# Block one's small inverses: transposed matrices by VectorE's block transpose, and seven more input pages in high and low halves

## The reference, cut to what matters

```python
h = rms_norm(x, norm1_g[l])
proj = h @ w_in[l]
p_rwkv, p_sb, q_mem, gate_logits = jnp.split(proj, cut, axis=-1)
...
def step(S, inp):                     # one token of the recurrence, 8 heads of 64 x 64
    r_t, w_t, k_t, v_t, kk_t, a_t = inp
    sa = jnp.einsum('bhij,bhj->bhi', S, -kk_t)
    S = S * w_t[:, :, None, :] + sa[..., None] * (kk_t * a_t)[:, :, None, :] + v_t[..., None] * k_t[:, :, None, :]
    y_t = jnp.einsum('bhij,bhj->bhi', S, r_t)
    return S, y_t
```

## Time and profile before

| | us |
|---|---|
| median of 3 runs (1365.85 to 1368.22) | 1367.03 |
| the profiled execution, whole time | 1366.13 |
| its span in the trace | 1364.3 |
| TensorE busy in it | 1269.6 |
| VectorE, ScalarE, GpSimd busy | 811.6, 673.0, 569.9 |

### The profile page before, as it was taken

How to read it: one execution, slowest core, us unless ns; L and a number is a source line. 1 busy time by engine, 2 the same in 40 slices (tenths; PEclk the granted TensorE clock), 3 DMA queues, 4 the chain that set the end, 5 groups by cost and what they waited for, 6 DMA issues and landing times.

```text
span 1364.3 us, 22840 instructions
## 1 busy us (share of the span) xinstructions
PE 1269.6 (93%) x8934; PEld 910.7 (67%) x8934; DVE 811.6 (59%) x1854; ACT 673.0 (49%) x1501; POOL 569.9 (42%) x385
## 2 busy tenths in 40 slices
PE   9999999999999999999999988888889888888786
PEld 7988897989999999997896543333434333333232
DVE  5845202464568773457338776666677666667755
ACT  4710233646566665564325564454555444554544
POOL 1100023516878888740005444444434444444342
PEclk9999999999999999999999999999999999999999
DMA  7432322425645556557539999999999999999997
GB/s 265 140 100 90 110 90 75 131 93 171 200 158 188 181 186 200 157 163 267 222 105 414 420 421 422 422 421 421 421 422 422 422 421 421 421 422 422 422 422 302
DMA packets 67940, 381.10 MB, mean 279 GB/s; under 512 B 7552, under 2 KB 7552, under 8 KB 35200
## 3 DMA queue, kind: packets, MB, share of 16 engines
q0 software_dynamic: 37296, 268.45, 47.4%
q1 hardware_dynamic: 29664, 107.84, 24.1%
q10 hardware_dynamic: 880, 3.41, 0.7%
HBM read 378.63 MB, written 1.05 MB: 278 GB/s over the span
## 4 chain that ended last, share of the span: by engine, by line
PE 58%; DMA 29%; ACT 5%; DVE 5%; issue 2%; POOL 0%; SPq 0%; POOLq 0%; DVEq 0%; ACTq 0%
DMA arena_block<-in_experts,arena_block 28%; PE bank L467 23%; PE bank L1111 9%; PE bank L503 5%; PE bank L521 3%; PE bank L465 2%; DVE arena_block L2490 2%; PE bank L1035 2%; PE bank L908 2%; PE bank L485 1%; PE bank L566 1%; DMA const<-in_const 1%; ACT arena_block L1721 1%; PE bank L1135 1%; PE bank L1045 1%
## 5 line engine op out<-in xcount | busy, mean ns | idle before, releaser
L1111 PE MATMUL bank<-arena_block 128*128 128x512 f32 x1012 | 485.4, 610 | 83.4 <-ACT arena_block L1721 81.8
L2627 POOL DMA_INDIRECT arena_block<-in_experts,arena_block x253 | 272.6, 1077 | 467.5 <-PE bank L1111 330.6
L2490 DVE SCALAR_TENSOR_TENSOR arena_block<-arena_block 128x1024 f32<-128x1024 f32 x256 | 314.1, 1227 | 188.5 <-DMA arena_block<-in_experts,arena_block 184.4
L1111 PEld LDWEIGHTS bank<-arena_block 128*128 128x128 f32 x1012 | 178.1, 190 | 350.2 <-ACT arena_block L1721 212.6
L2604 POOL TENSOR_TENSOR w_lo<-ring,w_hi 128x1024 fp32r<-128x1024 f32 x100 | 242.8, 2449 | 85.0 <-ACT w_hi L1219 84.7
L1715 ACT ACTIVATE arena_block<-arena_block 128x1 f32<-128x1 f32 x256 | 75.1, 293 | 278.8 <-DVE arena_block L2490 278.5
L1219 ACT ACTIVATE w_hi<-ring 128x1024 fp32r<-128x1024 f32 x112 | 117.8, 1054 | 51.6 <-PE bank L503 28.8
L467 PE MATMUL bank<-x_hi,w_hi 128*128 128x256 f32 x384 | 109.0, 284 | 0.0
L467 PE MATMUL bank<-x_hi,w_lo 128*128 128x256 f32 x384 | 108.7, 283 | 0.0
L467 PE MATMUL bank<-x_lo,w_hi 128*128 128x256 f32 x384 | 108.7, 283 | 0.0
L1721 ACT ACTIVATE arena_block<-const,arena_block 128x128 f32<-128x128 f32 x256 | 102.7, 401 | 8.3
(11 more groups left out here) (538 smaller groups left out, 2344.6 us busy)
## 6 DMA issues: line engine op xcount, KB each, us to landing
ring<-in_pages SPq DMA_DIRECT2D x175, 512.0 KB, 3.5
wq_pages<-in_pages SPq DMA_DIRECT2D x16, 512.0 KB, 4.4
arena_block<-in_experts,arena_block POOLq DMA_INDIRECT x259, 14.9
arena_block<-in_pages SPq DMA_DIRECT2D x8, 512.0 KB, 7.0
arena_mix<-in_memT ACTq DMA_DIRECT2D x1, 1024.0 KB, 9.0
arena_block<-in_subkT ACTq DMA_DIRECT2D x1, 1024.0 KB, 5.4
const<-in_const SPq DMA_DIRECT2D x1, 974.5 KB, 13.3
out_tok<-arena_block SPq DMA_DIRECT2D x3, 256.0 KB, 7.6
```

The lines of the kernel that those rows point to most:

```text
L1111: last = mm(bank[2 * tt + j][:, :], diag[:, slot, :], uv[slot][:, D + j * 512:D + (j + 1) * 512], start=start, stop=stop)
L2490: stt(uv[s][:, 0:D], uv[s][:, 0:D], 1.0, htok[:, tt, :], ALU.mult, ALU.mult, accum_out=e_act[:, s:s + 1])\
L2627: nc.gpsimd.indirect_dma_start(out=uv[slot], out_offset=None, in_=A["experts"], in_offset=bass.IndirectOffsetOnAxis(ap=eidx[:, n:n + 1], a ...
```

## The change

Three things change, all in block one between the first inverses and the first gate page.

1. **Transposes by DVE.** near_dt is gone. After DVE has added near_dd's product to DDn, one v.transpose of the whole 128 x 512 tile, which transposes each 32 x 32 block in place, writes DTn (STREAM_TRANSPOSE in the order). Side 1 of the first products is gone too: DDn is made as the transpose of DTn. Between the add and the transpose DVE waits for its own add (step).
2. **Seven more pages in halves.** in_a pages 19 to 25 get high halves by ACT (a_high, into w_hi rooms 0 and 1 in turn) and low halves by DVE (a_low). Pages 17 and 18 stay whole.
3. **The turns.** A level has two products instead of three, so four levels take pages 19 to 25 and one sbv page where they took seven in_a pages, four sbv and two mk pages. Each later step has the page of four places earlier beside it, and the four mv pages stand in one row between state and the first gate page.

```diff
-SHIFTED, ROWED, FIRST_SPLIT, SPLIT_END = 14, 5, 7, 17
-FIRSTS = list(range(PAGE0["in_a"] + FIRST_SPLIT, PAGE0["in_a"] + SPLIT_END))
+SHIFTED, ROWED, FIRST_SPLIT, SHIFTED_END, FROM_KEYS, SPLIT_END = 14, 5, 7, 17, 19, 26
+FIRSTS = list(range(PAGE0["in_a"] + FIRST_SPLIT, PAGE0["in_a"] + SHIFTED_END)) + list(range(PAGE0["in_a"] + FROM_KEYS, PAGE0["in_a"] + SPLIT_END))
...
-            return first_hi[page % SLOTS]
+            return first_hi[page % SLOTS if page < PAGE0["in_a"] + SHIFTED_END else page % 2]
...
         pe.wait_ge(S("b_dve"), B_DVE["scaled"])
-        for side in range(2):
-            if side:
-                a_page(18)
-            for c in range(2):
-                for h in range(8):
-                    j, ft, o = item(c, h)
-                    for b in range(0, P, NEAR):
-                        kb, ab = bT[o:o + 64, ft, c * P + b:c * P + b + NEAR], AR[o:o + 64, ft, c, 0, b:b + NEAR]
-                        at_ = side * T + (4 * c + ft) * NEAR
-                        last = mm(bank[4 + h % 2][b:b + NEAR, at_:at_ + NEAR], *((ab, kb) if side else (kb, ab)), start=True, stop=True)
+        for c in range(2):
+            for h in range(8):
+                j, ft, o = item(c, h)
+                for b in range(0, P, NEAR):
+                    last = mm(bank[4 + h % 2][b:b + NEAR, (4 * c + ft) * NEAR:(4 * c + ft + 1) * NEAR],
+                              bT[o:o + 64, ft, c * P + b:c * P + b + NEAR], AR[o:o + 64, ft, c, 0, b:b + NEAR], start=True, stop=True)
         last.then_inc(S("b_pe"), 1)
+        a_page(18)
...
-        for lv in range(2):
-            a_page(19 + 3 * lv)
+        for lv in range(4):
+            a_page(19 + 2 * lv)
             near_pp(lv)
-            pairs(3 * lv)
-            a_page(20 + 3 * lv)
+            pairs(2 * lv)
+            if lv < 3:
+                a_page(20 + 2 * lv)
+            else:
+                pe.wait_ge(S("norm_out"), 1)
+                linear("sbv", hn, by_token=True, part=(0, 1))
             near_dd(lv)
-            pairs(3 * lv + 1)
-            a_page(21 + 3 * lv)
-            near_dt(lv)
-            pairs(3 * lv + 2)
-        a_page(25)
-        near_pp(2)
-        pairs(6)
-        pe.wait_ge(S("norm_out"), 1)
-        linear("sbv", hn, by_token=True, part=(0, 1))
-        near_dd(2)
-        pairs(7)
+            pairs(2 * lv + 1)
         linear("sbv", hn, by_token=True, part=(1, 1))
-        near_dt(2)
-        linear("sbv", hn, by_token=True, part=(2, 1))
-        near_pp(3)
-        linear("sbv", hn, by_token=True, part=(3, 1))
-        near_dd(3)
-        pe.wait_ge(S("norm_out"), 2)
-        linear("mk", memn, part=(0, 1))
-        near_dt(3)
-        linear("mk", memn, part=(1, 1))
         pe.wait_ge(S("b_dve"), B_DVE["inv3"])
...
+        a_high(19)
         act.wait_ge(S("b_pe"), B_PE["bktok"])
...
         a_copy(18)
+        a_high(20)
...
+        a_copy(19)
+        a_high(21)
         for lv in range(4):
-            if lv == 3:
-                take("sbv", flat(sbv), part=(0, 3))
             act.wait_ge(S("b_pe"), B_PE[f"pp{lv}"])
             A_(PPn, two(bank[6][:, :], NEAR), ACT.Copy).then_inc(S("b_act"), 1)
-            if lv == 0:
-                a_copy(19)
-                a_copy(20)
-                a_copy(21)
-            if lv == 1:
-                a_copy(22)
-                a_copy(23)
-                a_copy(24)
-            if lv == 2:
-                a_copy(25)
-        take("sbv", flat(sbv), part=(3, 1))
-        take("mk", mk, part=(0, 2))
+            if lv < 3:
+                for b in (20 + 2 * lv, 21 + 2 * lv):
+                    a_copy(b)
+                    if b + 2 < SPLIT_END:
+                        a_high(b + 2)
+        take("sbv", flat(sbv), part=(0, 1))
...
             dve.wait_ge(S("b_pe"), B_PE[f"dd{lv}"])
-            dve.wait_ge(S("b_pe"), B_PE[f"dt{lv}"])
-            tt_(DDn, DDn, two(bank[7][:, :], NEAR), ALU.add)
-            tt_(DTn, DTn, two(bank[6][:, :], NEAR), ALU.add).then_inc(S("b_dve"), 1)
+            step(tt_(DDn, DDn, two(bank[7][:, :], NEAR), ALU.add))
+            v.transpose(near_flat(DTn), near_flat(DDn)).then_inc(S("b_dve"), 1)
...
-            stt(Cn[:, q::2, :], two(bank[4 + q][:, 0:T], NEAR), -1.0, half8(C_NEAR + 2 * NEAR), ALU.mult, ALU.mult)
-            last = stt(DDn[:, q::2, :], two(bank[4 + q][:, T:2 * T], NEAR), -1.0, half8(C_LOW1), ALU.mult, ALU.mult)
+            last = stt(Cn[:, q::2, :], two(bank[4 + q][:, 0:T], NEAR), -1.0, half8(C_NEAR + 2 * NEAR), ALU.mult, ALU.mult)
         done(dve, last, "b_dve", B_DVE["near_read"])
-        tt_(DTn, DTn, level(0), ALU.add)
-        tt_(DDn, DDn, level(0), ALU.add).then_inc(S("b_dve"), 1)
+        step(tt_(DTn, DTn, level(0), ALU.add))
+        v.transpose(near_flat(DDn), near_flat(DTn)).then_inc(S("b_dve"), 1)
+        a_low(19)
+        a_low(20)
         dve.wait_ge(S("b_act"), B_ACT["near_copied"])
         near_cross(1)
         pairs_read(0)
+        a_low(21)
+        near_add(0)
         pairs_read(1)
-        near_add(0)
+        a_low(22)
+        near_cross(2)
+        dve.wait_ge(S("in_a_copy"), SHIFTED_END - SHIFTED)
+        v.memset(DT, 0.0)
         pairs_read(2)
-        near_cross(2)
+        a_low(23)
+        near_add(1)
         pairs_read(3)
-        dve.wait_ge(S("in_a_copy"), SPLIT_END - SHIFTED)
-        v.memset(DT, 0.0)
-        norm_apply(1, mem_raw, "mem_g", memn)
+        a_low(24)
+        near_cross(3)
         pairs_read(4)
-        near_add(1)
+        a_low(25)
+        near_add(2)
         pairs_read(5)
-        near_cross(3)
+        dve.wait_ge(S("in_a_copy"), N_IN_A - SHIFTED - 4)
+        tt_(sq_of["sbq"], sbq, sbq, ALU.mult)
         pairs_read(6)
         dve.wait_ge(S("in_a_copy"), N_IN_A - SHIFTED)
-        tt_(sq_of["sbq"], sbq, sbq, ALU.mult)
+        norm_apply(1, mem_raw, "mem_g", memn)
+        near_add(3)
         pairs_read(7)
-        near_add(2)
         tt_(sq_of["sbk"], sbk, sbk, ALU.mult)
         tt_(sq_of["mq"], mq, mq, ALU.mult)
-        near_add(3)
```

More of the change, by code:

```diff
@@ L98, in numbered @@
     return {n: i + 1 for i, n in enumerate(names.split())}
-B_PE = numbered("lora_up gate_up kk_sum kk_spread bonus_up vtok near bktok pp0 pairs0 dd0 pairs1 dt0 pairs2 pp1 pairs3 dd1 pairs4 "
-                "dt1 pairs5 pp2 pairs6 dd2 pairs7 dt2 pp3 dd3 dt3 pp32 dd32 pp64 dd64 g0 u0 y0 state g1 u1 y1 gn_mean qk_sum "
+B_PE = numbered("lora_up gate_up kk_sum kk_spread bonus_up vtok near bktok pp0 pairs0 dd0 pairs1 pp1 pairs2 dd1 pairs3 "
+                "pp2 pairs4 dd2 pairs5 pp3 pairs6 dd3 pairs7 pp32 dd32 pp64 dd64 g0 u0 y0 state g1 u1 y1 gn_mean qk_sum "
                 "gn_var sbq_spread gn_spread mk_spread z0 z1 cum0 cum1 sbo score mem_flip mem_out")
@@ L548, in a_page @@
                     pe.wait_ge(S("hn_low_early"), 1)
-                if b < FIRST_SPLIT or b >= SPLIT_END:
+                if PAGE0["in_a"] + b not in FIRSTS:
                     linear("in_a", hn, part=(b, 1))
@@ L576, in near_dd @@
             near_product(7, DTn, PPn).then_inc(S("b_pe"), 1)
-        def near_dt(lv):
-            near_product(6, PPn, DTn).then_inc(S("b_pe"), 1)
         def pairs(j):
@@ L731, in _ @@
         last.then_inc(S("b_pe"), 1)
-        linear("mk", memn, part=(2, 1))
+        linear("sbv", hn, by_token=True, part=(2, 1))
         pe.wait_ge(S("b_act"), B_ACT["pp32"])
@@ L740, in _ @@
         last.then_inc(S("b_pe"), 1)
-        linear("mk", memn, part=(3, 1))
+        linear("sbv", hn, by_token=True, part=(3, 1))
         pe.wait_ge(S("b_dve"), B_DVE["dd32"])
@@ L746, in _ @@
         last.then_inc(S("b_pe"), 1)
-        linear("mv", memn, by_token=True, part=(0, 1))
+        pe.wait_ge(S("norm_out"), 2)
+        linear("mk", memn, part=(0, 1))
         pe.wait_ge(S("b_act"), B_ACT["pp64"])
@@ L751, in _ @@
         last.then_inc(S("b_pe"), 1)
-        linear("mv", memn, by_token=True, part=(1, 1))
+        linear("mk", memn, part=(1, 1))
         pe.wait_ge(S("b_dve"), B_DVE["pairs7"])
         chunk_g(0)
-        linear("mv", memn, by_token=True, part=(2, 1))
+        linear("mk", memn, part=(2, 1))
         pe.wait_ge(S("b_act"), B_ACT["dd64"])
         chunk_u(0)
-        linear("mv", memn, by_token=True, part=(3, 1))
+        linear("mk", memn, part=(3, 1))
         chunk_y(0)
@@ L765, in _ @@
         last.then_inc(S("b_pe"), 1)
+        linear("mv", memn, by_token=True)
         pe.wait_ge(S("hn_high"), 1)
@@ L1351, in _ @@
         last.then_inc(S("b_act"), 1)
+        take("sbv", flat(sbv), part=(1, 1))
         act.wait_ge(S("b_pe"), B_PE["pp32"])
@@ L1356, in _ @@
         last.then_inc(S("b_act"), 1)
-        take("mk", mk, part=(2, 1))
+        take("sbv", flat(sbv), part=(2, 1))
         act.wait_ge(S("b_pe"), B_PE["dd32"])
@@ L1362, in _ @@
         last.then_inc(S("b_act"), 1)
-        take("mk", mk, part=(3, 1))
+        take("sbv", flat(sbv), part=(3, 1))
         act.wait_ge(S("b_pe"), B_PE["pp64"])
@@ L1369, in _ @@
```

(15 more changed lines are left out.)

2 lines of the change are left out of this document (1 added, 1 removed).

## The result

| | before | changed |
|---|---|---|
| median, us | 1367.70 (6 runs, 1365.85 to 1368.93) | 1356.97 (6 runs, 1355.42 to 1357.60) |
| the profiled execution, us | 1366.13 | 1355.61 |
| its span, us | 1364.3 | 1353.8 |
| TensorE busy, us | 1269.6 | 1259.5 |
| VectorE, ScalarE busy, us | 811.6, 673.0 | 818.7, 680.1 |

The ratio is 0.992 with a 95% interval of 0.9907 to 0.9932: faster by 10.7 us, where the prediction had 1356.9 us for the median and 1354.1 us for the span. A second set of five runs gave 1356.62 us.

What follows compares the result with a forecast made beforehand. TensorE was taken to bound the kernel up to 560 us. Removing 4.88 + 1.22 + 4.06 = 10.16 us from the profiled 1366.13 gives 1355.97; with 0.90 added, the median is 1356.9 us, range 1354.6 to 1361.2.

Steps and rivals of the forecast that it cites:

- What bounds it: Up to 560 us TensorE bounds the kernel; a microsecond off it there should come off the end.
- What goes: TensorE time removed: near_product 4.88 us, side 1 of the first products 1.22, seven pages in halves 4.06; sum 10.16.
- The transpose: Price of one 128x512 transpose on DVE, taken as the add's 0.69 us; no row showed one.
- The tightest place: Page 19: its low half ready at 82.4 us, TensorE there at 82.86; slack 0.4 us, no wait.
- The mv row: Four mv pages before the first gate page, 15.1 us; that page's low half ready 3.6 us early.
- The gaps left in: Two unexplained TensorE stops in near_product, 0.63 and 0.52 us, assumed to remain.
- Starves for instructions: Rival: TensorE's gaps in runs of smallest products multiply, 3.6 to 4.8 us come back: 1361.1 us; chance 0.10.
- The slow transpose: Rival: a transpose takes 3.5 us, page 19 and following groups wait, 4.0 us come back: 1360.9 us; chance 0.07.
- the slower case: Rival: transposes bound each level; at 7 us each, net 7.4 us slower, 1374.3 us; chance 0.03.
- Given back: Rival: after 256 us, loads at their own pace absorb the earlier start: 1367.0 us; chance 0.04.

Runs made afterwards that it cites:

- the kernel with the whole pages: Changed kernel with in_a pages 19 to 25 whole again, transposes and turns kept: 1359.32 us.
- the kernel with the products apart: Changed kernel with the five transposes made by TensorE products again, each level's near_dt behind the pairs group instead of right behind near_dd: 1379.32 us.
- the densest kernel: Changed kernel with the five transposes made by TensorE products again, near_dt right behind near_dd, halves and turns kept: 1385.01 us.

## Why the prediction was right

- *What bounds it.* Right. The stretch is TensorE's, and a microsecond off it came off the end: the first gate page starts at 180.84 instead of 191 us, 10.4 us earlier, and the span ends 10.5 us earlier.
- *What goes.* near_product, 1024 records of the same 1.22 us a group: 4.88. Side 1: 1.22. The pages: page 19 3.46 to 2.86 and six times 3.65 to 3.06, 4.14 where 4.06 were taken. Sum 10.24 against 10.16.
- *The transpose.* 0.71 us against 0.69, both in the bare row and, five times over, as 0.75 us from start to start. The estimate of 1.24 us from the Trainium skill's "VectorE: DVE Perf Modes", "The three transpose paths", doesn't hold here: the measurement decides. VectorE's busy time rose by 7.1 us (about 8 foretold), ScalarE's by 7.1 (7.3).
- *The tightest place.* Slack 0.41 us, as worked out. It was tight enough that two more pages ahead of it fill it. Page 23 had 1.13 us (its low half ends at 102.57, the page starts at 103.70) where 1.4 were foretold.
- *The mv row.* Ready 3.3 us early against 3.6. The row takes 14.49 us, not 4 x 3.77 = 15.1 as the prediction had it. Before, the four mv pages were not all at 3.77 either: 3.77, 3.77, 3.63 and 3.63, 14.80 us. So the row gains 0.31 us, and the four mk pages that moved between the small products another 0.28 (3.65, 3.65, 3.51 and 3.51 us where they were four times 3.65).
- *The gaps left in.* They didn't stay as they were: 1.15 became 1.52 us, at other places, and the restarts of split pages and groups 0.38 became 0.83: 0.82 us lost.
- *What the sum didn't have.* Besides 0.31 and 0.28 us, the transposes of bT and kT take 0.87 instead of 1.02 us ahead of a page in halves (0.15), the step for 32 rows 1.13 instead of 1.18 (0.05), and the stretch began 0.17 us earlier by chance. 10.24 + 0.31 + 0.28 + 0.15 + 0.05 + 0.17 - 0.82 = 10.38, and the first gate page comes 10.38 us earlier. Misses of 0.8 and 1.0 us of opposite sign hide behind a forecast of 10.16; that it fits the median to 0.1 us is luck.
- *The rivals.* "Starves for instructions" had the right mechanism, but not the size: beside the kernel with the whole pages it cost this change 2.35 us of the halves' 4.1, beside the kernel before 0.82, not 3.6 to 4.8. The slow transpose and the slower case were wrong on the price of the transpose alone: five and ten times over they came, by their own places. (By its own sum the slower case ends at 1374.5 us, not 1374.3.) Given back: the last window shows nothing of it.

What the prediction didn't see is why the change is worth having in this order. It priced the transposes as 6.1 us of TensorE's time. Against the same order with the products left in, they are worth 28.

## What to carry to other kernels

Price a removed TensorE group by its time on the chain, but when you reorder, count instructions too. Here every gap stood behind 256 instructions that had run in less than 3.8 us; two groups of 256 small instructions need a page of long products between them, and eight medium ones aren't enough. A wait or a gap of 2 us on TensorE cost nearly as much again behind it, in work at the lower clock, so a forecast of a wait needs that second term. And when an edit is worth one microsecond, look first at what slips by itself from run to run.

## What the runs showed of the hardware

- *Supply of instructions.* TensorE's list comes in packets of 16 KB, 1.06 MB in 65 packets for 16944 instructions. All 28 gaps sit at 256 k + 193 instructions, move with 128 added ones, and end 1.12 to 1.58 us after packet k has landed; the packets took 0.88 to 1.63 us. The largest gap, 3.59 us, is in the densest kernel. This is the Trainium skill's rule, "Runtime: NRT & Kernel Launch", "Instruction fetch mechanics", that engines fetch in blocks of 256 while they run the block before. Its "mostly hidden" holds for long products and fails for small ones: 10.6 us of gaps in the kernel with the products apart.
- *The clock behind an idle.* After 1.86 us of standing still 21 products of a page took 4.17 us; after 0.88 us, and in the kernel with the products apart after 1.49 us, the same 21 took 2.67. After 1.99 us a whole page took 5.34 instead of 3.65, with a granted clock of 0.68 between 81.50 and 86.85 us, a mean of the levels of 1.2 and 2.4 GHz.
- *VectorE's block transpose* of 128x512 f32 takes 0.71 us, as much as an add.
- Open: why the clock falls in some executions at a page near 56 us with no idle ahead of it, and why an instruction packet goes out sooner or later behind the same instruction.
